# A weight unit's low part is split off two k-steps after its high part

## The reference

```python
h = rms_norm(x, norm_mix); z = h @ w_in          # first block: 34 column tiles of 128
y_a = windowed_gqa(...); y_b = neighborhood_attn(...)
x = x + (gate_a * (y_a @ w_proj_a) + gate_b * (y_b @ w_proj_b)) @ w_out
x = x + square(relu(rms_norm(x, norm_mlp) @ w_up)) @ w_down        # 4096 wide: 32 tiles
x = rms_norm(x, norm_final)
for l in range(2):                                                 # second block
    x = x + 0.5 * (silu(h @ wg) * (h @ wu)) @ wd                   # 2816 wide: 22 tiles
    x = x + concat(sliding_window_attention, short_conv) @ w_out   # h = rms_norm_2(x)
    x = x + 0.5 * (silu(h @ wg) * (h @ wu)) @ wd
return rms_norm_2(x, final_norm)
```

## Time and profile before

| | |
|---|---|
| device time, median of 3 runs | 2550.73 us (2550.05 to 2551.12) |
| the profiled execution | 2552.07 us, its span 2550.3 us |
| PE busy | 2510.3 us, 98% |
| DVE, ACT, POOL busy | 1240.5, 886.2, 276.7 us |
| DVE on w_lo (L1066) | 387 instructions, 483.8 us |
| ACT on w_hi (L870) | 438 instructions, 451.9 us |
| POOL on w_lo (L1305) | 51 instructions, 122.2 us |

### The profile page before, as it was taken

The page is one execution under the profiler, slowest core; times in us unless marked ns, Lnnn a source line. Parts: engine busy times, 40 slices in busy tenths (PEclk is TensorE's granted clock), DMA queues, the critical chain, the costliest instruction groups (busy, mean ns, idle before and its releaser), DMA issues.

```text
span 2550.3 us, 28074 instructions
## 1 busy us (share of the span) xinstructions
PE 2510.3 (98%) x11494; PEld 2072.8 (81%) x11494; DVE 1240.5 (49%) x1524; ACT 886.2 (35%) x1329; POOL 276.7 (11%) x194
## 2 busy tenths in 40 slices
PE   7999999999999999999999999999999999999997
PEld 6887888888888888878888888888888788888886
DVE  5544455434365343465554444543434655544444
ACT  5555434223253222345332222422223444322222
POOL 4242110000030000014200000100000133000002
PEclk9999999999999999999999999999999999999998
DMA  5111333233223333231233332333332322333322
GB/s 163 51 59 50 99 116 98 92 99 99 91 85 105 99 99 93 83 107 59 91 92 99 99 100 85 99 98 99 98 101 83 93 75 75 99 99 95 99 92 70
DMA packets 69423, 235.36 MB, mean 92 GB/s; under 512 B 8752, under 2 KB 11440, under 8 KB 69296
## 3 DMA queue, kind: packets, MB, share of 16 engines
q1 hardware_dynamic: 67632, 230.36, 29.1%
q0 software_dynamic: 1664, 3.22, 0.6%
HBM read 231.35 MB, written 2.19 MB: 92 GB/s over the span
## 4 chain that ended last, share of the span: by engine, by line
PE 90%; DVE 4%; ACT 3%; issue 2%; POOL 0%; DMA 0%; SPq 0%; DVEq 0%; ACTq 0%; POOLq 0%
PE bank L758 28%; PE bank L760 28%; PE bank L759 28%; PE bank L799 2%; PE bank L772 2%; DVE w_lo L1066 2%; PE bank L786 1%; ACT w_hi L870 1%; DVE x L1167 1%; ACT z L861 0%; POOL square_sum L1315 0%; DVE q L1123 0%; DVE z L1058 0%; PE bank L810 0%; PE bank L832 0%
## 5 line engine op out<-in xcount | busy, mean ns | idle before, releaser
L758 PE MATMUL bank<-h_hi,w_hi 128*128 128x512 f32 x2224 | 883.3, 397 | 10.8 <-DVE w_lo L1066 9.4
L760 PE MATMUL bank<-h_hi,w_lo 128*128 128x512 f32 x2224 | 868.6, 391 | 0.0
L759 PE MATMUL bank<-h_lo,w_hi 128*128 128x512 f32 x2224 | 868.2, 390 | 0.0
L1066 DVE TENSOR_TENSOR w_lo<-w_raw,w_hi 128x1024 fp32r<-128x1024 f32 (+1 forms) x387 | 483.8, 1251 | 327.8 <-ACT w_hi L870 327.4
L870 ACT ACTIVATE w_hi<-w_raw 128x1024 fp32r<-128x1024 f32 (+1 forms) x438 | 451.9, 1034 | 413.0 <-PE bank L760 410.4
L758 PEld LDWEIGHTS bank<-h_hi,w_hi 128*128 128x128 f32 x2224 | 419.0, 188 | 97.7 <-DVE w_lo L1066 10.8
L760 PEld LDWEIGHTS bank<-h_hi,w_lo 128*128 128x128 f32 x2224 | 418.6, 188 | 88.7
L759 PEld LDWEIGHTS bank<-h_lo,w_hi 128*128 128x128 f32 x2224 | 419.4, 189 | 81.1 <-issue 2.0
L760 PE MATMUL bank<-act_hi,w_lo 128*128 128x512 f32 x960 | 373.4, 389 | 0.0
L758 PE MATMUL bank<-act_hi,w_hi 128*128 128x512 f32 x960 | 373.4, 389 | 0.0
L759 PE MATMUL bank<-act_lo,w_hi 128*128 128x512 f32 x960 | 373.4, 389 | 0.0
(11 more groups left out here) (163 smaller groups left out, 1668.8 us busy)
## 6 DMA issues: line engine op xcount, KB each, us to landing
w_raw<-ffn_wg_dram SPq DMA_DIRECT2D x88, 512.0 KB, 3.5
w_raw<-ffn_wu_dram SPq DMA_DIRECT2D x88, 512.0 KB, 3.5
w_raw<-w_in_dram SPq DMA_DIRECT2D x70, 512.0 KB, 3.5
w_raw<-ffn_wd_dram SPq DMA_DIRECT2D x64, 512.0 KB, 3.5
w_raw<-w_up_dram SPq DMA_DIRECT2D x32, 512.0 KB, 3.5
w_raw<-w_down_dram SPq DMA_DIRECT2D x32, 512.0 KB, 3.8
w_raw<-w_out_dram SPq DMA_DIRECT2D x24, 512.0 KB, 3.5
w_raw<-ffn_wd_dram SPq DMA_DIRECT2D x32, 384.0 KB, 3.1
```

Source lines behind the costliest of these rows:

```text
L758: engine.matmul(to, w_hi[s][:, lhs], hi, start=k == 0, stop=False)
L759: engine.matmul(to, w_hi[s][:, lhs], lo, start=False, stop=False)
L760: product = engine.matmul(to, w_lo[s][:, lhs], hi, start=False, stop=job == "k_last")
L1066: engine.tensor_tensor(lo, value, hi.bitcast(F32), ALU.subtract).then_inc(signals[event].s, 1)
```

## The change

The split becomes two jobs. `split_hi` (ACT) stays where the split was; `split_lo` (DVE's `split_v` or POOL's `split_g`) is put in two slots later. In `dense_first` both stand together for the first three units, as before.

```diff
     SIGNALS = {
-        "fetch": (), "split_v": ("w_hi", "w_lo_v"), "split_g": ("w_hi", "w_lo_g"), "k_step": (), "k_last": (),
+        "fetch": (), "split_hi": ("w_hi",), "split_v": ("w_lo_v",), "split_g": ("w_lo_g",), "k_step": (), "k_last": (),
...
     def run(self, job, key):
-        if job == "split":
-            self.split(*key)
+        if job == "split_lo":
+            self.split_lo(*key)
+            return
+        if job == "split_hi":
+            self.add(job, *key)
             return
...
-    def split(self, u):
+    def split_lo(self, u):
         self.lo_by[u] = "w_lo_g" if self.split_job == "split_g" else "w_lo_v"
         self.add(self.split_job, u)
...
             self.add("fetch", u + UNITS_HELD)
-            self.later(slots, "split", u + UNITS_HELD)
+            self.later(slots, "split_hi", u + UNITS_HELD)
+            self.later(slots + 2, "split_lo", u + UNITS_HELD)
...
             if k < UNITS_HELD:
-                self.split(k)
+                self.add("split_hi", k)
+                self.split_lo(k)
...
             for job, key, r, zs in jobs:
-                if job in ("split_v", "split_g"):
+                if job == "split_hi":
                     u = key
```

## The result

The changed kernel takes **2562.85 us** (median of 5 runs, 2562.13 to 2563.46), the kernel before in the same session 2550.73 (2549.86 to 2551.89). The ratio is 1.0046, with an interval of 1.0036 to 1.0057: 12.1 us slower. The profiled execution after took 2562.51 us with a span of 2560.7, that is 10.4 more than the span before.

What follows compares the result with a forecast made beforehand. PE, busy 2510.3 us of a 2550.3 us span, was taken as the bound. The terms 1.1 + 4.8 + 2.7 = +8.6, plus 3.4 for the clock, put 2550.73 at 2562.7 us, range 2555 to 2567.

Steps and rivals of the forecast that it cites:

- Which low parts move: Of 438 units, 425 cross no job; on DVE one moves at the start and two after each of five dense_pair calls.
- The start, +1.1: First norm: unit 4's low part falls behind the reciprocal, so PE's wait for the first score grows by 1.1 us.
- The 6-wide pairs, 3 x 1.6: Three 6-wide pairs before a norm: PE waits some 2.5 us for a low part at m = 3; net +1.6 each.
- The 8-wide pair, +2.7: First MLP, near 707: PE waits 1.8 us, residual 2 starts 2.3 later, the loop to the norm decides: +2.7 us.
- POOL in DVE's way: At the pairs, POOL's addition starts 0.10 us before DVE comes free and delays the 6-wide pairs' first low part by 1.10.
- The clock, +3.4: After two of the three new 2.5 us waits the granted clock falls, costing 1.7 us each: +3.4 us.
- the sum without the clock: Whole kernel: the start, the 6-wide pairs and the 8-wide pair together, +8.6 us.
- Rival 4: First scores: low parts fall behind stack_lo, three PE waits shrink about 1.1 us each, two clock falls may go: -6.7; chance 0.02.
- Rival 2: Pairs: DVE beats POOL to the port, +5.8; second sum, with no exclusion at all, +3.2; chance 0.12.

Runs made afterwards that it cites:

- run 1: Changed kernel, but the low parts of the two units following each dense_pair stand directly behind their high parts again: 2552.16 us, ratio 1.0005.
- run 2: Changed kernel, but only the low parts after a dense_pair are late, by four slots; all others directly behind their high parts: 2561.85 us, ratio 1.0043.
- run 3: Changed kernel, but low parts directly behind their high parts, those after a dense_pair between residual 0 and h_tile 0: 2548.44 us, in a second session 2547.46.
- run 4: Changed kernel, with four filler products on PE before its wait for the late low part after the first four pairs: 2563.54 us.
- run 6: Changed kernel, but POOL's addition of the second tile's squares waits for both late low parts after the first four pairs: 2554.87 us, ratio 1.0016.
- run 5: Changed kernel, with three filler products on PE before the late low part's wait at 6-wide pairs, two at the 8-wide one: 2559.75 us, ratio 1.0038.
- run 8: Changed kernel, but ordinary low parts three slots late instead of two, behind stack_lo; pairs and start as in the change: 2546.90 us, ratio 0.9987.
- run 7: Changed kernel, but low parts after a dense_pair behind residual 0, ordinary ones three slots late, first units' directly behind their high parts: 2533.59 us, ratio 0.9934.

## Why the prediction was right, and where not

The forecast was 2562.7 us, the measurement 2562.85. The mechanism came as told, at the places and nearly with the waits that were foreseen. That the numbers agree to 0.15 us is partly luck: the 3.4 us for the clock is a count of falls, and half of them came in another place. Term by term:

- **Which low parts move.** Right. Runs 1 and 2 show it from both sides: without the pairs the cost is gone, with the pairs alone it is there.
- **The start, +1.1.** The first score came 1.05 later, as reckoned. In the one trace after it is given back by the second norm (-0.1), for two reasons. The clock came back at 62.1 there and at 62.2 before, so that after a longer wait fewer products ran slowly: (5.46 - 4.28) / 2 = 0.6. And the trace before is itself slow later on: from PE's wait at 124.3 to the second sum of squares it takes 266.6 us, and 266.1 in all ten other traces; its granted clock read 0.95 in that stretch and 1.00 in theirs, but that this is the reason isn't shown. Over the traces the term is real: from the first to the second sum of squares take 365.0, 363.3, 364.4 and 364.5 us in the four kernels with the old order of the start (before, runs 2 and 3, run 3 again), on average 364.3, and 365.0, 365.5, 365.3, 365.3 and 365.7 in the five with the new one (after, runs 1, 4, 6 and 5), on average 365.3: +1.0. Two of the four are odd, before by its slow stretch and run 2 with 3.4 us of half clock at the start where the others have 6.8; with 0.5 off the first and without the second it is +0.9. The medians of run 1 (+1.0) agree, though none of these is beyond the doubt of one run.
- **The 6-wide pairs, 3 x 1.6.** Residual 0, h_hi 0 and the 0.10 us of POOL's lead came as reckoned, the wait of 2.5 measured 2.45. Net of the clock the norm's sum came later by +1.5, within 0.1 of the term: 4.3 (after) - 2.9 (the lateness of `scaled_sum`'s product in the first MLP, 741.50 before and 744.40 after) = 1.4 at the second pair, 3.2 - 1.7 = 1.5 at the third, 1.5 at the fourth. Run 8, without a fall, gives 1.5, 1.6 and 1.5.
- **The 8-wide pair, +2.7.** Residual 2 was foreseen 2.3 later than before, the wait of PE at 1.8: it measured 1.79. From the second to the third norm's sum it is +2.7 in run 8, with the same wait and no fall, just the term, and +3.3 in the changed kernel, where the clock fell. So of the 1.7 us of that fall 0.6 showed and the rest hid behind the loop: "mostly", as foreseen, not wholly.
- **POOL in DVE's way.** Run 6 bears it out: what DVE lost (1.07 us per pair, for an overlap of 1.21) was POOL's. That the one that comes second loses is seen in the first MLP of the kernel after. POOL's first addition came before the low part and took its usual 1.3 us; its second one came behind DVE and took 2.26 instead of 1.29:

```profile
706.77 4.52 DVE L1071 TENSOR_TENSOR w_lo<-w_raw,w_hi 128x1024 fp32r<-128x1024 f32 x2
```

```profile
706.67 1.31 POOL L1320 TENSOR_TENSOR square_sum<-square_sum,z 128x512 f32<-128x512 f32 x1 [317.70 <-ACT z L866]
707.95 2.26 POOL L1320 TENSOR_TENSOR scaled_sum<-scaled_sum,z 128x512 f32<-128x512 f32 x1
```

- **The clock, +3.4.** The size fits but isn't measured closely: the run with PE kept busy (run 5) is 8.7 above the kernel before, where the sum without the clock was 8.6, with a median that is uncertain by some 3 us. Within run 8 alone, executions with the lower mean clock took up to 4.8 us more. Of the trace's full falls that the trace before hadn't, I had the number right and one place wrong: one, not two, of the three waits of 2.45 was followed by one; one came after the scores of layer 1 instead, where the trace before had none. In run 2 all of the three were followed by one, in run 8's trace none. It is a matter of the single execution, and a forecast can only give it a mean.
- **Rival 4 was rightly unlikely for this change and wrongly priced.** The step that failed is "each would shrink by one low part of about 1.1 us": the low part's own length isn't what stands ahead of `stack_lo`, but its wait for ACT (4.51 and 2.42 us at the start, up to 3.7 in the later layers). Crossing `stack_lo` is worth 13.9 us (run 7 against run 3 in the same session) or 16.3 (run 8 against the change), not 6.7, and it was one slot away. The expectation of run 7 repeated the mistake, with the belief that the two waits of 2.2 us hang on other things; they went too.
- **A slip in a sum.** Rival 2's second sum is 1.1 + 1.5 + 0.7 = 3.3, not 3.2, which changes nothing.

Left open: why the clock falls after one wait of 2.2 or 2.45 us and not after another of the same length. And nothing was tried on the low part at 32.40 that still stands ahead of the first evacuations.

## What to carry to other kernels

To see what a move in a common list of jobs does, write down for each engine what it is moved past on its own queue: here 425 of 438 moves were nothing, eight cost 11 us with the clock and one about 1, and one slot more moved ten others and won 14 to 16. An instruction that waits for another engine blocks its queue for the whole of that wait, so put it behind everything that is ready, but not behind what is itself due only after the next buffer is needed; the best place is the gap in which the engine is idle anyway. And look at what the moved instruction lands beside: over half of the harm, with the falls of the clock that came of it, was due to an addition on POOL that began 0.1 us earlier.

## What the runs showed of the hardware

- A subtraction on DVE with two inputs in SBUF and an addition on POOL with two inputs there didn't share: the one that came 0.10 us later waited for the other (two low parts in 2.89 us against 1.82 without the addition beside them, run 6). An addition that came second took 2.26 us instead of 1.29 (the first MLP of the kernel after).
- In the wait at the first score the granted clock fell to 0.50. It came back at 62.2 us where PE resumed at 56.76 (before), and at 62.1 where it resumed at 57.81 (after), so a later start made the slow work shorter, 4.28 us instead of 5.46. That is no rule: PE resumed at 57.82 in run 1 and at 59.45 in run 5, and the clock came back at 63.1 and 65.4, 5.3 and 5.9 us later.
- Four products of float32 `ones` with 512 columns of float32 took 3.0 us from the first start to the next product's (run 4), 0.76 each, at a granted clock of 1.00, against 0.23 for a product of split parts.
